# The first two down projections of the first feed-forward as one product in seven halves

## The reference

```python
hn = rmsnorm(h, norm2_g[l])
up = causal_dwconv(jnp.einsum("bsd,df->bsf", hn, ffn_w_up[l]), ffn_conv_w[l]) + ffn_conv_b[l]
f_gate, f_val = jnp.split(up, [D_FF], axis=-1)
h = h + jnp.einsum("bsf,fd->bsd", jax.nn.silu(f_gate) * f_val, ffn_w_down[l])
return rmsnorm(h, final_g)
```

## Time and profile before

| | us |
|---|---|
| median of 3 executions | 2140.8 (2138.76 to 2141.86) |
| the profiled execution, its own time | 2137.23 |
| its span in the profile | 2135.0 |
| TensorE busy | 2118.7, 99% of the span |
| VectorE, ScalarE, GpSimd busy | 1483.1, 1047.9, 543.3 |
| TensorE's granted clock over the span | 0.999 of 2.4 GHz |
| the first feed-forward in the profile | about 596 to 958 us |

### The profile page before, as it was taken

One profiled execution on the slowest core, in us unless ns is written; L12 is line 12 of the kernel. 1 busy time (PEld: TensorE's weight loads), 2 busy tenths in 40 slices (PEclk: granted clock), 3 DMA queues, 4 the chain that ended last, 5 costly groups with the idle time before them and its releaser, 6 DMA issues.

```text
span 2135.0 us, 31735 instructions
## 1 busy us (share of the span) xinstructions
PE 2118.7 (99%) x11828; PEld 1821.1 (85%) x11828; DVE 1483.1 (69%) x2421; ACT 1047.9 (49%) x1851; POOL 543.3 (25%) x450
## 2 busy tenths in 40 slices
PE   9999999999999999999999999999999999999998
PEld 6777898888888888888887899999887778999897
DVE  7768334687578485776777587878666785868775
ACT  6876443436432222253777354554445763545543
POOL 2100431143322021143665231200222222311012
PEclk9999999999999999999999999999999999999999
DMA  8887312444676686533445357995322334555673
GB/s 266 252 242 216 99 57 73 168 158 166 230 195 158 176 190 167 142 105 98 159 176 170 113 177 219 284 259 187 99 96 82 89 74 125 174 183 186 201 194 128
DMA packets 140281, 348.89 MB, mean 163 GB/s; under 512 B 38113, under 2 KB 42465, under 8 KB 126817
## 3 DMA queue, kind: packets, MB, share of 16 engines
q1 hardware_dynamic: 123840, 235.19, 33.8%
q0 software_dynamic: 9360, 68.69, 15.2%
q10 hardware_dynamic: 6928, 42.99, 5.6%
HBM read 333.71 MB, written 115.87 MB: 211 GB/s over the span
## 4 chain that ended last, share of the span: by engine, by line
PE 92%; DVE 3%; ACT 2%; issue 1%; DVEq 0%; POOLq 0%; POOL 0%; DMA 0%; SPq 0%; ACTq 0%
PE bank L422 9%; PE bank L423 9%; PE bank L426 9%; PE bank L542 8%; PE bank L545 8%; PE bank L543 8%; PE bank L935 5%; PE bank L939 5%; PE bank L937 5%; PE bank L441 3%; PE bank L440 3%; PE bank L439 3%; PE bank L2463 1%; PE bank L1729 1%; PE bank L2490 1%
## 5 line engine op out<-in xcount | busy, mean ns | idle before, releaser
L336 ACT ACTIVATE b_wh<-b_raw 128x1024 fp32r<-128x1024 f32 (+2 forms) x313 | 323.0, 1034 | 616.9 <-PE bank L426 341.3
L347 DVE TENSOR_TENSOR b_wl<-b_raw,b_wh 128x1024 fp32r<-128x1024 f32 (+2 forms) x270 | 341.4, 1265 | 111.7 <-ACT b_wh L336 109.0
L542 PE MATMUL bank<-b_xh,b_wh 128*128 128x512 f32 x712 | 295.1, 414 | 0.5 <-DVE b_wl L347 0.4
L543 PE MATMUL bank<-b_xl,b_wh 128*128 128x512 f32 x712 | 278.0, 390 | 0.0
L545 PE MATMUL bank<-b_xh,b_wl 128*128 128x512 f32 x704 | 275.9, 392 | 0.0
L1142 POOL TENSOR_TENSOR b_yl<-b_arena,b_yh 128x512 fp32r<-128x512 f32 x50 | 78.4, 1568 | 589.4 <-ACT b_yh L1053 355.9
L422 PE MATMUL bank<-b_xh,b_wh 128*128 128x512 f32 x504 | 197.2, 391 | 0.1
L423 PE MATMUL bank<-b_xl,b_wh 128*128 128x512 f32 x504 | 196.3, 389 | 0.0
L426 PE MATMUL bank<-b_xh,b_wl 128*128 128x512 f32 x496 | 193.3, 390 | 0.0
L347 POOL TENSOR_TENSOR b_wl<-b_raw,b_wh 128x1024 fp32r<-128x1024 f32 (+1 forms) x45 | 104.0, 2310 | 219.5 <-ACT b_wh L336 187.2
L545 PEld LDWEIGHTS bank<-b_xh,b_wl 128*128 128x128 f32 x704 | 132.1, 188 | 29.3
(11 more groups left out here) (565 smaller groups left out, 5291.4 us busy)
## 6 DMA issues: line engine op xcount, KB each, us to landing
scr_sums<-in_quarters POOLq DMA_DIRECT2D x32, 1024.0 KB, 9.1
scr_sums<-in_quarters ACTq DMA_DIRECT2D x28, 1024.0 KB, 5.0
b_more_raw<-scr_sums SPq DMA_DIRECT2D x108, 256.0 KB, 3.1
b_raw<-scr_sums SPq DMA_DIRECT2D x100, 256.0 KB, 3.4
scr_sums<-scr_sums POOLq DMA_DIRECT2D x20, 1024.0 KB, 8.7
b_raw<-in_quarters SPq DMA_DIRECT2D x80, 256.0 KB, 3.0
b_more_raw<-in_quarters SPq DMA_DIRECT2D x76, 256.0 KB, 3.0
scr_sums<-in_quarters ACTq DMA_DIRECT2D x7, 1536.0 KB, 6.7
```

Source lines behind the costliest of these rows:

```text
L336: act.activation(panel_hi_lo(n)[0][:, cols], raw_of(n)[:, cols], ACT.Copy).then_inc(w_hi, 1)
L347: dve.tensor_tensor(lo, raw_of(n)[:, cols], hi.bitcast(F32), ALU.subtract).then_inc(w_lo, 1)
L542: pe.matmul(bank[:, :], ph[:, w], hi[:, x, :], start=(k == 0), stop=False)
L543: last = pe.matmul(bank[:, :], ph[:, w], lo[:, x, :], start=False, stop=(n in SIDE_BY_SIDE and k == kt - 1))
```

## The change

`c0dn` and `c1dn` go through `down_seven` like s and m: 8 + 20 panels instead of 8 + 8. Two more raw buffers (in the arena) and split tiles (the former spare ones) serve these 28 panels, in the order extra, extra, ordinary, ordinary. Outside these segments the c panels keep two buffers. The weight sums grow by 8 pairs, two pieces of 1 MB for each of four sums, which come first in the order of pieces: 8 more copies and 8 more accumulating copies in all. In c's up projections the last tap with its bias goes from VectorE to ScalarE.

```diff
-        ("c0up", 16, 8), ("c0dn", 8, 8), ("c1up", 16, 8), ("c1dn", 8, 8), ("c2up", 12, 8), ("c2dn", 8, 6),
+        ("c0up", 16, 8), ("c0dn", 8, 8), ("c1up", 16, 8), ("c1dn", 20, 8), ("c2up", 12, 8), ("c2dn", 8, 6),
-SEVEN_PAIRS = 36 + 16
+SEVEN_PAIRS = 36 + 24
+for _seg in ("c0dn", "c1dn"):
+    for _i in range(CNT[_seg]):
+        _n = BASE[_seg] + _i
+        BUFFER[_n] = (2, 3, _n % 2, _n % 2)[_i % 4]
...
-        SPARE = {BASE[f"c{ch}dn"] + 1 + i: i for ch in range(3) for i in range(2)}
+        SPARE = {BASE["c2dn"] + 1 + i: i for i in range(2)}
+        c_raw = take(36 * T, 2, DT * P)
...
                 if f == 0 and i == 0:
                     pe.wait_ge(out_free, n)
                 if f == 2 and i == 0:
                     pe.wait_ge(bank_copied, bank_copied0[l] + 2)
-                if f == 3 and i == 4:
+                if l == "c" and f == 5 and i == 12:
+                    pe.wait_ge(out_free, base)
+                if l != "c" and f == 3 and i == 4:
...
+                    dve.wait_ge(first_tap, first_tap0 + 2 * p + r + 1)
+                    return conv_taps(dve, scaled, dst, 3, lambda j: V("fconv", c * 3 + j), False)
+
+                def product():
                     dve.drain()
                     dve.wait_ge(gate_silu, p + 1)
                     wait(dve, y_ready, q + YR[l] + first)
                     dve.tensor_tensor(product_of(l, ch, q), sg, cv, ALU.mult).then_inc(prod_done, 1)
+
+                def value():
+                    taps()
+                    product()
+                    if ch == 1:
+                        for part in range(3):
+                            m = down_sum(dve, l, q, part)
+                        if q == 7:
+                            m.then_inc(sums_lo, 1)
+
+                def gate():
+                    taps().then_inc(gate_conv, 1)
+
+                def convolved():
+                    (gate, value)[r]()
+                    if ch == 2 and t < 10:
+                        add_down(dve, l, t)
+                if l == "c":
+                    return convolved
...
             split_and(dve, split_lo, f"{l}{ch}up", post, True)
+            for n in range(BASE[f"c{ch}dn"] + 2, BASE[f"c{ch}dn"] + 4):
+                if l == "c" and n in DOWN_OF:
+                    split_lo(dve, n, 0, n % 2, KT_OF[n])
...
+                if l == "c":
+                    c = q + (first + r * FT)
+                    act.wait_ge(out_free, n + 1)
+                    act.activation((cg, cv)[r], raws[r], ACT.Identity, bias=V("fbias", c), scale=V("fconv", c * 3 + 2))\
+                        .then_inc(first_tap, 1)
+                if r == 1:
                     if l == "c":
                         act.wait_ge(gate_conv, q + (first + 1))
...
+                if t in (18, 19):
+                    b = t - 18
+                    dve.tensor_tensor(out[:, 2 * b, :], t21[:, b, :], u_kept[:, b, :], ALU.subtract).then_inc(down_read, 1)
+                    m = dve.tensor_tensor(out[:, 2 * b + 1, :], p7[:, b, :], u_kept[:, b, :], ALU.add)
+                    if t == 18:
+                        m.then_inc(down_read, 1)
+                    else:
+                        m.then_inc(out_free, CNT[f"{l}1dn"] + (CNT[f"{l}0dn"] if l != "c" else 0))
             for ch in range(3):
                 hidden_dve(dve, "c", ch, "norm2" if ch == 0 else None)
-                split_and(dve, split_lo, f"c{ch}dn", add_to_h(dve, "an0", "an0f") if ch == 2 else add_to_h(dve), True)
+                split_and(dve, split_lo, f"c{ch}dn", (None, down_parts, add_to_h(dve, "an0", "an0f"))[ch], ch == 2)
...
-                products_down(pe, f"c{ch}dn", lambda k: (y_ready, YR["c"] + PAIRS[ch][0] + k + 1))
+                if ch < 2:
+                    down_seven(pe, f"c{ch}dn")
+            products_down(pe, "c2dn", lambda k: (y_ready, YR["c"] + PAIRS[2][0] + k + 1))
```

More of the change, by code:

```diff
@@ L445, in down_seven @@
             l, second = seg[0], seg[1] == "1"
[L446 to L447 removed]
+            base, tiles = BASE[seg], DOWN_TILES[l]
+            read = sum(SEVEN[f"{l}1st"][2:4]) if l != "c" else 0
             for i in range(CNT[seg]):
@@ L697, in build, with __init__, product @@
         h_quarter = h[:, :, :].rearrange("p t (b j c) -> p j b t c", b=NB, j=4)
[L701 to L706, removed]
+        class DownTiles:
+            def __init__(self, name, kept, kept_lo, third_at, p1, p7, t21, banks):
+                self.kept, self.kept_lo, self.banks = kept, kept_lo, banks
+                self.third, self.third_lo = take(third_at, 8, T // 2), operands(f"{name}_lo2", arena_at + 4 * third_at, 8, T // 2)
+                self.p1, self.p7, self.t21, self.out = take(p1, 2, T), take(p7, 2, T), take(t21, 2, T), kept[0]
+            def product(self, k):
+                return self.kept[k // 4][:, k % 4, :]
@@ L738, in conv_taps @@
                 d = width - 1 - j
-                dve.drain()
+                if ins is not None:
+                    dve.drain()
                 ins = dve.scalar_tensor_tensor(out=dst[:, d:T], in0=bank[:, 0:T - d], scalar=tap(j),
@@ L832, in hidden_act @@
             if l == "c":
+                for n in range(BASE[f"c{ch}dn"] + 2, BASE[f"c{ch}dn"] + 4):
+                    if n in DOWN_OF:
+                        split_hi(act, n, 0, n % 2, KT_OF[n])
                 product_hi(cnt - 1)
@@ L957, in gated @@
                     .then_inc(prod_done, 1)
[L959 to L964, removed]
-                    return dve.tensor_tensor(x0, x0, x1, ALU.subtract)
-                return dve.tensor_tensor(third[:, q, :], pr[:, T0], x0, ALU.subtract)
             if ch == 2:
@@ L2973, in _, with first_banks, down_sums @@
             split_and(act, split_hi, "wout", with_copies)
+            def first_banks(n, t, q, r, bank):
+                l = layer_of(n)
+                if t == 5 and l == "s":
+                    act.wait_ge(r_ang, 1)
+                if t == 5:
+                    act.wait_ge(mm_done, BASE[f"{l}0dn"] + 4)
+                    tiles = DOWN_TILES[l]
+                    for b in range(2):
+                        m = act.activation(tiles.p1[:, b, :], pb[tiles.banks[0][b]][:, :], ACT.Copy)
+                        if l == "c" and b == 0:
+                            m.then_inc(out_free, CNT["c0dn"])
+                        else:
+                            m.then_inc(bank_copied, 2 if l == "c" else 1)
+            def down_sums(n, t, q, r, bank):
+                l = layer_of(n)
+                base, tiles = BASE[f"{l}1dn"], DOWN_TILES[l]
+                if t == 0:
+                    act.wait_ge(mm_done, BASE[f"{l}0dn"] + 8)
+                    for b in range(2):
+                        act.activation(tiles.p7[:, b, :], pb[tiles.banks[1][b]][:, :], ACT.Copy).then_inc(bank_copied, 1)
+                if t == 5:
+                    act.wait_ge(sums_lo, sums_lo0[l] + 1)
+                    act.wait_ge(mm_done, base + 4)
+                if t in (5, 6):
+                    dst, tokens = ((yh, T1), (yl, T0))[t - 5]
+                    for x in range(2):
+                        act.activation(dst[:, 4 * x:4 * x + 4, T0], tiles.kept[x][:, :, tokens], ACT.Copy).then_inc(sums_hi, 1)
+                if t == 9:
+                    act.wait_ge(mm_done, base + 8)
+                    for x in range(2):
+                        act.activation(yl[:, 4 * x:4 * x + 4, T1], tiles.third[:, 4 * x:4 * x + 4, :], ACT.Copy)\
+                            .then_inc(sums_hi, 1)
             act.wait_ge(s_gain, 1)
```

233 lines of the change are left out of this document (115 added, 118 removed).

## The result

| | before | after |
|---|---|---|
| median, lowest to highest, us | 2138.81, 2136.91 to 2141.86 (20 runs) | 2142.11, 2139.27 to 2149.12 (20 runs) |
| ratio after to before, 95% interval | | 1.0018, 1.0011 to 1.0025 |
| profiled execution, its span, us | 2137.23, 2135.0 | 2142.15, 2140.3 |
| matmuls on TensorE | 11828 | 12116 |
| HBM read, written, MB | 333.71, 115.87 | 356.78, 132.64 |

The change makes the kernel slower by 0.18%, 3.9 us with an interval of 2.4 to 5.3 us; the medians lie 3.3 apart. The forecast of 2141.4 us and its range hold the measured time, and "the same" within 0.2% is what came out by the bound of the prediction.

A forecast was written before the change was run, and what follows sets the result against it. TensorE, busy 99% of the span, was taken as the bound. A saving of 6.40 us less new waits of 0.94, 2.2 and 3.84 gave +0.6 us: 2141.4 us against the median 2140.8, range 2137.4 to 2145.6.

The forecast's parts named there:

- The saving: c0dn and c1dn: 672 matmuls of 256 columns replace the 512-column ones, 80.64 instead of 87.04 us, 6.40 saved.
- wait 1: Start of c0dn: first panel in halves waits for the last up panel's eviction, 0.94 us lost, range 0.9 to 1.3.
- wait 2: Third panel of c1dn: TensorE waits for VectorE's low part, queued behind half sums, 2.2 us, range 1.3 to 3.2.
- wait 3: c1dn to c2up: first panel waits for recombination queued behind the second panel's split, 3.84 us, range 3.8 to 4.3.
- The sum. -6.40 + 0.94 + 2.2 + 3.84: Whole kernel: saving plus three new TensorE waits, +0.6 us on the profiled 2137.23, giving 2141.4 us against the median.
- The seven more additions in s fall where GpSimd is nearly idle: In s: added weight-sum additions cost nothing, since GpSimd is busy only 4.0 of 57.6 us.
- The tap: c's up projections: ScalarE's 44 operations of about 0.8 us are covered; VectorE in c1up becomes about 67.5 us busy.
- (1): c1dn to c2up: the wait for recombination is not there; 2137.5 us, counted as no difference, chance 0.11.
- (2): c1dn's third panel and c2up's start: both waits are hidden; 2135.3 us, faster, chance 0.07.
- (3): c1up: VectorE becomes the bound, 0.7 us over in each of 8 pairs, 5.6 us more, 2147 us, chance 0.08.
- (4): c1dn and s1dn: panel loads fall behind, 5 us over 20 panels, 2146 us, slower, chance 0.04.
- (5): c's up projections: a 1.28 us table load at each change between tap and silu, 2144 us, chance 0.02.

The follow-up runs named there:

- experiment 6: Changed kernel with its three TensorE waits reordered away and no weight-sum additions beside s0st (five beside s2st, one behind its last pair): 2134.15 us, ratio 0.9979.
- the repeat: The changed kernel run and profiled once more, unaltered: 2141.85 us, ratio 1.0017 to the kernel before.
- experiment 3: Changed kernel with the last tap back on VectorE: 2150.14 us, ratio 1.0050 to the kernel before.
- experiment 5: Changed kernel reordered against its three TensorE waits: recombinations and third-panel split earlier, c0dn's first panel awaiting one eviction fewer: 2135.45 us, ratio 0.9983.
- Experiment 1: Changed kernel with VectorE's recombinations in c1dn's last two steps ahead of the splits of c2up's panels: 2137.69 us, ratio 0.9996.
- experiment 2: Changed kernel with VectorE's split of c1dn's third panel ahead of the last half sums of c1up: 2140.99 us, ratio 1.0010.
- experiment 4: Changed kernel without weight-sum additions beside s0st, two made behind it and six each beside s1st and s2st: 2141.84 us, ratio 1.0015.
- experiment 7: Kernel before with one wait added, c2up's first panel waiting for the low part of its second: 2142.55 us, ratio 1.0016.

## Why the prediction was right or wrong

**The saving, right.** 6.40 us: 23.10 and 57.6 us after, against 23.04 and 57.60. In experiment 6 c as a whole came out 6.2 us shorter.

**Waits 1, 2 and 3, right.** 0.94, 2.2 and 3.84 were forecast, 0.99, 2.22 and 3.83 came. VectorE's eviction, which the forecast has behind wait 1, is not named there by the waits; by the timeline it ends at 686.47 and TensorE starts at 686.58. The terms that had no row of their own can be checked in VectorE's timeline behind c1up:
```profile
802.18 1.34 DVE L1068 TENSOR_TENSOR b_arena<-b_arena 128x256 f32<-128x256 f32 x1
803.45 2.35 DVE L355 TENSOR_TENSOR b_wl<-b_raw,b_wh 128x1024 fp32r<-128x1024 f32 x2
```
The last half sum takes 1.34 instead of 0.42 us beside GpSimd's low part, the 0.9 us that the earlier trace rows lent to wait 2.

**"The sum. -6.40 + 0.94 + 2.2 + 3.84", wrong by a missing term.** The step took each matmul behind a wait at the 0.227 us of the earlier trace rows and so priced a wait by its length alone. The clock's column in the windows of the kernel before read 1.00 in all five stretches, but TensorE had never stood still there for more than 0.5 us; a wait of 3.8 us was outside what those rows could speak for. The term is 2.5 and 1.7 us in the changed kernel's two traces, and 1.7 in the kernel before with a wait of 2.67. It was not even a bound or a rival. The upper bound has a slip of its own: the upper ends of the three waits, 1.3, 3.2 and 4.3, less 6.40 are +2.4 and not +2.9. Nothing hangs on it.

**"The seven more additions in s fall where GpSimd is nearly idle", wrong.** They cost GpSimd nothing, but its time was not what they take. The cover named was of the wrong resource: the panels' loads wait, ScalarE waits for a load, and its bank copy is queued behind. s grew by 2.1 us in the profiled execution and by 1.7 in the repeat. The prediction named this as what would make it wrong. By place it is shown by six traces with and four without; in the total it is not, since moving the additions only brought gaps elsewhere.

**Where they add up.** In the profiled execution: -6.40 + 0.99 + 2.22 + 3.83 + 2.5 = +3.1 in c. Measured are +2.5, since some 0.7 us of small waits of before are gone or hidden in c0up and c1up. With +2.1 in s that is 4.6 us, and the 0.8 ahead of c0up make the spans 5.3 apart. In the repeat c is 1.7 us longer than before, s 1.7 and m 1.6, and the spans lie 5.0 apart. The execution profiled before was 1.6 us under its median, which is why these differences are above the 3.3 of the medians.

**The number was luck.** By the medians the sum of +0.6 is short by 2.7 us. The base, 2140.8, was the median of only three runs and 2.0 us above that of twenty. The two errors all but cancel, and so the forecast stands 0.7 us from the measured time.

**The tap, right.** The taps on ScalarE by source line:
```profile
L873 ACT ACTIVATE b_arena<-b_arena,b_vec x44: 797/802/819, 606.4 to 929.2; 128x512 f32<-128x512 f32 x44
```
44 of 0.80 us, as estimated, and no table load on their line. The Trainium skill (ScalarE: Activation LUTs, "Table sets: the hidden batching unit") has identity in every set. For silu's set this trace agrees: silu has three table loads in the whole kernel, as before. VectorE in c1up was to be busy 67.5 us; it is 70.65, 3 us more, without effect.

**The rivals.** (1) and (2) did not come: waits 2 and 3 stand in every trace of the changed kernel. (3) did not come in the changed kernel, but in experiment 3, with the tap back, four pairs are up to 1.05 us late, the first two with VectorE at work without a pause. So the tap's move was needed, although late loads can bring gaps of the same size without it (experiment 5). (4), loads that fall behind, was placed in c1dn and s1dn. There it did not come: TensorE's waits in c1dn name no load, and s1dn is 57.60 again. It came instead in s0st, and in some executions in c1up. (5) did not come.

**Experiment 1's own expectation** missed 0.96 us by the same oversight as the kernel: moving the last operations ahead of their split leaves them behind the split of the step before.

## What to carry to other kernels

Where TensorE never rests, price a new wait by its length and by the matmuls behind it: here waits of 2.7 us and more cost another 1.7 to 2.6 us at half clock, and 1 us cost 0.1. If no row of the trace has such a wait, put that into the range as a bound. When a scheme is moved to a place with fewer buffers, look at the operations that release what the next stage waits for, and take them ahead of any split that waits for a buffer; one line of order was worth 4.4 us, more than half of all that the new scheme saves. And name the cover of a moved transfer by what it competes with, the loads of the panels, rather than by the idle time of the engine that issues it.

## What was not expected of the hardware

The granted clock fell to 0.50 at one stop of TensorE in an otherwise full stream. It did so at all five waits of 3.83 us in the traces (after, its repeat, experiments 2, 3 and 4), at one of 3.7 (experiment 3) and at the 2.67 us put into the kernel before. At 2.22 us it did so in one trace of four (experiment 4), and at 0.96 us not. The length of the wait is not all, since experiment 3 shows one more such place at 157 us, in an earlier stage, behind a gap of only 1.2 us.

The same wait of 3.83 us cost 1.7 us more in two traces (the repeat and experiment 2) and 2.5 to 2.6 in three (after, experiments 3 and 4). The traces show what differs. In the three the clock fell while TensorE still stood, in the two only after it had started again. In the changed kernel it fell at 858.8, ahead of the start at 860.48, and in the repeat at 861.2, behind the start at 859.83. One window of each around the fall:
```profile
858.00:859.00 1.00, 0.00 (x0) 0.00 (x0) 1.00 (x1) 0.00 (x0) 0.00 (x0) 0.91 0.97 369
861.00:862.00 1.00, 1.00 (x5) 0.77 (x4) 0.00 (x0) 0.00 (x0) 0.00 (x0) 0.60 0.11 41
```
The wait of 2.67 us was of the second kind (fall at 863.2, start at 862.94), and so was the one of 2.22 (1.6 us more). What sets the moment of the fall is open.

The accumulating transfers and the panels' loads share something that the mean DMA share does not show. s1dn runs without a gap at 0.88 (after) and at 0.94 (before), while s0st has gaps at 0.83 to 0.85 with two additions beside it. Nor is every gap the change's: experiment 7, with the kernel before's additions, has one of 0.6 us in s1dn. Which queue or which transfer holds the late load up was not tried.
